# Split products of a two-layer hybrid block: both activation parts in one 512-column product, halves summed by VectorE, and the gated product moved from GpSimd to VectorE

## What is computed

```
for layer in range(2):
    mod = silu(c) @ ada_w[layer] + ada_b[layer]        # six vectors of 2048: shift, scale, gate
    h = rms_norm(x) * (1 + sc_m) + sh_m
    y = even_mixer(h) or odd_mixer(h)                  # projections, mLSTM + forgetting attention, or GLA
    x = x + g_m * rms_norm(y)
    h = rms_norm(x) * (1 + sc_f) + sh_f
    u = conv3(h @ ffn_in_w) + conv_b                   # 2048 -> 2 * 5632, causal depthwise convolution, 3 taps
    a, g = split(u)
    y = (a * gelu(g)) @ ffn_out_w                      # 5632 -> 2048
    x = x + g_f * rms_norm(y)
```

## Time and profile before

| | |
|---|---|
| median of 3 runs | 2530.39 us (2529.86 to 2533.49) |
| the profiled execution | 2531.67 us, its span 2529.9 us |
| mean granted TensorE clock | 0.981 |
| TensorE (PE) busy | 2439.9 us, 96% |
| VectorE (DVE) busy | 1929.7 us, 76% |
| ScalarE (ACT) busy | 999.6 us, 40% |
| GpSimd (POOL) busy | 427.1 us, 17% |
| DMA | 627.17 MB, mean 248 GB/s |

### The profile page before, as it was taken

The page is one execution under the profiler, slowest core; times in us unless marked ns, Lnnn a source line. Parts: engine busy times, 40 slices in busy tenths (PEclk is TensorE's granted clock), DMA queues, the critical chain, the costliest instruction groups (busy, mean ns, idle before and its releaser), DMA issues.

```text
span 2529.9 us, 39852 instructions
## 1 busy us (share of the span) xinstructions
PE 2439.9 (96%) x15954; PEld 2232.7 (88%) x15954; DVE 1929.7 (76%) x2371; ACT 999.6 (40%) x1012; POOL 427.1 (17%) x199
## 2 busy tenths in 40 slices
PE   7999999899999999999999899999999999999998
PEld 5878787789987999799879889987999899988996
DVE  6769888889987999799877676677999466655665
ACT  2133344343333334333444444455433333333343
POOL 0000000014420443024200000000344024410430
PEclk9999999999999999999989999999999999999999
DMA  9989866947788777887858744455677555555553
GB/s 386 412 321 348 311 238 222 325 174 273 273 303 307 277 273 286 323 291 274 302 190 300 241 149 144 149 212 204 250 273 258 194 188 183 182 184 197 181 183 136
DMA packets 114474, 627.17 MB, mean 248 GB/s; under 512 B 12768, under 2 KB 12960, under 8 KB 63152
## 3 DMA queue, kind: packets, MB, share of 16 engines
q1 hardware_dynamic: 113648, 621.22, 67.3%
q10 hardware_dynamic: 704, 4.23, 0.4%
HBM read 623.27 MB, written 2.13 MB: 247 GB/s over the span
## 4 chain that ended last, share of the span: by engine, by line
PE 79%; DVE 10%; DMA 8%; ACT 2%; issue 1%; SPq 0%; DVEq 0%; POOL 0%; ACTq 0%
PE bank L1702 15%; PE bank L1703 15%; PE bank L1704 15%; PE bank L1727 8%; PE bank L1728 8%; PE bank L1729 8%; DMA piece<-ada_pieces 7%; PE bank L1508 4%; DVE lo L920 3%; DVE piece L931 3%; ACT hi L502 1%; PE bank L1614 1%; PE bank L1487 1%; PE bank L1520 1%; DMA extra<-blocks_in 0%
## 5 line engine op out<-in xcount | busy, mean ns | idle before, releaser
L502 ACT ACTIVATE hi<-raw 128x2048 fp32r<-128x2048 f32 x378 | 723.6, 1915 | 1183.8 <-PE bank L1704 734.3
L1702 PE MATMUL bank<-act,hi 128*128 128x256 f32 x3616 | 1032.9, 286 | 12.1 <-DVE lo L920 10.0
L1703 PE MATMUL bank<-act,hi 128*128 128x256 f32 x3616 | 1026.8, 284 | 0.0
L1704 PE MATMUL bank<-act,lo 128*128 128x256 f32 x3616 | 1026.6, 284 | 0.0
L920 DVE TENSOR_TENSOR lo<-raw,hi 128x2048 fp32r<-128x2048 f32 x378 | 864.8, 2288 | 203.5 <-ACT hi L502 202.7
L1702 PEld LDWEIGHTS bank<-act,hi 128*128 128x128 f32 x3616 | 697.8, 193 | 17.8 <-DVE lo L920 12.8
L1703 PEld LDWEIGHTS bank<-act,hi 128*128 128x128 f32 x3616 | 697.7, 193 | 0.3
L1704 PEld LDWEIGHTS bank<-act,lo 128*128 128x128 f32 x3616 | 697.5, 193 | 0.0
L931 DVE SCALAR_TENSOR_TENSOR piece<-piece,cond 128x1024 f32<-128x1024 f32 x290 | 413.8, 1430 | 79.7 <-DMA piece<-ada_pieces 79.5
L901 POOL TENSOR_TENSOR region<-region 128x256 f32<-128x256 f32 x88 | 205.4, 2334 | 1012.4 <-ACT region L805 1012.4
L1727 PE MATMUL bank<-hi,mid 128*128 128x512 f32 x704 | 277.0, 393 | 9.3 <-DVE lo L920 9.3
(11 more groups left out here) (176 smaller groups left out, 1707.6 us busy)
## 6 DMA issues: line engine op xcount, KB each, us to landing
raw<-w_units SPq DMA_DIRECT2D x378, 1024.0 KB, 4.8
piece<-ada_pieces SPq DMA_DIRECT2D x290, 512.0 KB, 4.8
region<-ada_pieces SPq DMA_DIRECT2D x64, 512.0 KB, 11.3
raw<-head_units SPq DMA_DIRECT2D x16, 1024.0 KB, 11.5
y<-ada_pieces SPq DMA_DIRECT2D x30, 512.0 KB, 5.6
region<-gamma_scratch ACTq DMA_DIRECT2D x4, 1024.0 KB, 6.6
x<-x_in SPq DMA_DIRECT2D x1, 2048.0 KB, 9.3
x_out<-x SPq DMA_DIRECT2D x3, 512.0 KB, 2.8
```

The costliest lines, as they stand in the source:

```text
L502: sc.activation(hi[:, slot, :], raw[:, raw_slot, :], ACT.Copy).then_inc(s_hi, 1)
L1702: pe.matmul(dst, w_hi, act[:, kt, 0:T], start=at == 0, stop=False)
L1703: pe.matmul(dst, w_hi, act[:, kt, T:2 * T], start=False, stop=False)
L1704: i_ = pe.matmul(dst, w_lo, act[:, kt, 0:T], start=False, stop=at == DK - 1)
```

## The change

- In all column stages but the gates, L1702 and L1703 become one product with 512 streaming columns, `act[:, kt, :]`, into the whole bank; w_lo x act hi still adds to the first 256 columns.
- The two halves are summed when the bank is evacuated: TENSOR_REDUCE with add over a view of the bank as 256 pairs, each pair 256 elements apart. In the other column stages it takes the place of the copy; in `ff_up` it writes `ff_sum` in SBUF, and the three convolution steps read that in place of the bank, after one more own wait.
- GpSimd's L901 and L904 move to VectorE's queue, behind `lo`: `ff_product` in even iterations, `mid_low` in odd ones, and both behind the first `lo` of the `ff_down` that follows.

```diff
@@ in gpsimd
-                if ph.kind == "ff_up":
-                    def body(i, ph=ph):
...
-                            gp.tensor_tensor(ff_m[:, slot, :], conv_a[:, slot, :], gelu_g[:, slot, :],
-                                             ALU.mult).then_inc(s_mul, 1)
-                            gp.wait_ge(s_mh, p)
-                            gp.tensor_tensor(flat(mid[:, at_, T:2 * T]), ff_m[:, slot, :],
-                                             flat(mid[:, at_, 0:T].bitcast(F32)), ALU.subtract).then_inc(s_mid, 1)
@@ in vector
+            def ff_product(ph, q, slot):
+                ve.wait_ge(s_gelu, ph.pairs + q + 1)
+                if not isinstance(q, int) or ph.pairs + q >= 2:
+                    ve.wait_ge(s_mid, ph.pairs + q - 1)
+                ve.tensor_tensor(ff_m[:, slot, :], conv_a[:, slot, :], gelu_g[:, slot, :], ALU.mult).then_inc(s_mul, 1)
+
+            def mid_low(ph, q, slot):
+                ve.wait_ge(s_mh, ph.pairs + q + 1)
+                at_ = bass.ds(q, 1)
+                ve.tensor_tensor(flat(mid[:, at_, T:2 * T]), ff_m[:, slot, :], flat(mid[:, at_, 0:T].bitcast(F32)),
+                                 ALU.subtract).then_inc(s_mid, 1)
@@ in vector, after lo of the next unit and before the piece
+                        if ph.kind == "ff_up" and not (first_body(i) and j < 2):
+                            q = 2 * i + (j // 2 - 1)
+                            (ff_product if j % 2 == 0 else mid_low)(ph, q, (j // 2 + 1) % 2)
+                        if ph.kind == "ff_down" and first_body(i) and j == 0:
+                            ff_product(last_up, 2 * last_up.bodies - 1, 1)
+                            mid_low(last_up, 2 * last_up.bodies - 1, 1)
@@ in vector, the evacuation
+                        tile_parts = bank[2 * (tile_no % 2)][:, :].rearrange("p (b t) -> p t b", b=2)
...
-                            ve.tensor_copy(region[:, bass.ds((ph.dest + ph.units * i + j) * T, T)], tile_ps)\
-                              .then_inc(s_evac, 1)
+                            ve.tensor_reduce(region[:, bass.ds((ph.dest + ph.units * i + j) * T, T)], tile_parts, AX_X,
+                                             ALU.add).then_inc(s_evac, 1)
...
-                            ve.tensor_scalar(out_, tile_ps, vec[:, bass.ds(ch + 2, 1)], vec[:, bass.ds(ch + 3, 1)],
+                            ve.wait_ge(s_evac, 2 + ph.t0 + i * ph.tiles + tile)
+                            ve.tensor_reduce(ff_sum, tile_parts, AX_X, ALU.add).then_inc(s_v, own.tick())
+                            mine()
+                            ve.tensor_scalar(out_, ff_sum, vec[:, bass.ds(ch + 2, 1)], vec[:, bass.ds(ch + 3, 1)],
                                              ALU.mult, ALU.add).then_inc(s_v, own.tick())
                             mine()
-                            ve.scalar_tensor_tensor(out=out_[:, 1:T], in0=tile_ps[:, 0:T - 1],
+                            ve.scalar_tensor_tensor(out=out_[:, 1:T], in0=ff_sum[:, 0:T - 1],
...
-                            ve.scalar_tensor_tensor(out=out_[:, 2:T], in0=tile_ps[:, 0:T - 2],
+                            ve.scalar_tensor_tensor(out=out_[:, 2:T], in0=ff_sum[:, 0:T - 2],
@@ in tensor, columns
-                    dst = bank[2 * ((ph.t0 + j) % 2)][:, 0:T]
+                    both = bank[2 * ((ph.t0 + j) % 2)][:, :]
+                    dst = both[:, 0:T]
...
-                        pe.matmul(dst, w_hi, act[:, kt, 0:T], start=at == 0, stop=False)
-                        pe.matmul(dst, w_hi, act[:, kt, T:2 * T], start=False, stop=False)
+                        if ph.kind == "gates":
+                            pe.matmul(dst, w_hi, act[:, kt, 0:T], start=at == 0, stop=False)
+                            pe.matmul(dst, w_hi, act[:, kt, T:2 * T], start=False, stop=False)
+                        else:
+
+                            pe.matmul(both, w_hi, act[:, kt, :], start=at == 0, stop=False)
                         i_ = pe.matmul(dst, w_lo, act[:, kt, 0:T], start=False, stop=at == DK - 1)
```

More of the change, by code:

```diff
@@ L175 @@
 REGION = V_AT + TB * D
-OWN = {("ff_up", None): 8, ("columns", "fox"): 6, ("values", "fox"): 12, ("columns", "mlstm"): 14,
+OWN = {("ff_up", None): 12, ("columns", "fox"): 6, ("values", "fox"): 12, ("columns", "mlstm"): 14,
        ("values", "gla"): 8, ("columns", "gla"): 8}
@@ L273, in program @@
                                         for k in range(4))
+        ff_sum = extra[:, 0:T]
         diag = split2(region[:, V_AT:V_AT + T])
@@ L860, in _ @@
             gp.memset(zeros, 0.0).then_inc(s_zeros, 1)
-            gp.sem_inc(s_mul, 2)
             for ph in PHASES:
@@ L894, in _ @@
                         stage_values(h)
-                if ph.kind == "ff_up":
-                    def body(i, ph=ph):
[L897 to L900, removed]
-                            gp.tensor_tensor(ff_m[:, slot, :], conv_a[:, slot, :], gelu_g[:, slot, :],
-                                             ALU.mult).then_inc(s_mul, 1)
-                            gp.wait_ge(s_mh, p)
-                            gp.tensor_tensor(flat(mid[:, at_, T:2 * T]), ff_m[:, slot, :],
-                                             flat(mid[:, at_, 0:T].bitcast(F32)), ALU.subtract).then_inc(s_mid, 1)
-                    repeat(gp, ph, body)
         @block.vector
@@ L1301, in _ @@
             ve.sem_inc(s_pair, 2)
+            ve.sem_inc(s_mul, 2)
             ve.sem_inc(s_mod, 2)
@@ L1469, in _ @@
                     own.at = base + per * ph.bodies
+                if ph.kind == "ff_up":
+                    last_up = ph
                 def between(ph=ph):
```

## The result

| | before | after |
|---|---|---|
| median | 2530.12 us (4 runs, 2528.17 to 2533.49) | 2557.66 us (4 runs, 2554.84 to 2565.55) |
| ratio to before [95% interval] | | 1.0112 [1.0086, 1.0138] |
| the profiled execution, its span | 2531.67, 2529.9 us | 2554.84, 2553.1 us |

The change makes the kernel slower by 27.5 us at the median and by 23.2 us between the two profiled executions, 1.1%. The forecast was 2547.5 us, +17.1, with slower the likeliest: the sign and the mechanism hold, the size was 6 to 10 us short.

The account below looks back on a forecast made before the run. TensorE and VectorE stood within 3% of each other in 120 of 176 `ff_up` units. Terms 27.4 + 0.5 - 11.9 - 3.4 + 2 + 1.5 + 1 gave +17.1 us, a median of 2547.5, range 2533 to 2563.

Parts of the forecast that it names:

- VectorE's cycle: Looped `ff_up` units with a piece: VectorE needs 6.12 us against TensorE's 5.76 before, so +27.4 us over 76 units.
- the piece's stall: VectorE's piece in `ff_up`: 0.54 us of its 1.76 read as waiting for GpSimd, going with GpSimd's work.
- the own wait behind the reduce: VectorE's loops: the one added wait on its own past work lengthens the reduce's 0.69 us by 0.15.
- Straight units: The 44 `ff_up` units with a piece outside loops: VectorE needs 5.77 us, +0.01 each, +0.5 us in all.
- TensorE's part: Column units: one 512-column matmul at 0.227 us replaces two at 0.240, 16 times, saving 0.21 us: 5.55 a unit.
- the 120 units with a piece: `ff_up` units with a piece, looped and straight: VectorE becomes last, +27.9 us forecast.
- the 56 without: `ff_up` units without a piece: TensorE stays last and each saves 0.21 us, -11.9 us.
- Fox and mLSTM: Their 16 column units: engines alternate as last, between -3.4 and +4.3 us, taken as +1.5.
- Rival 1: `ff_up` units with a piece: VectorE's cycle fits under TensorE's and the kernel gets faster, 2495 us; chance 0.15.
- Rival 2: VectorE's convolution steps in `ff_up` cost 0.42 us each from SBUF, giving 2532 us, no change; chance 0.10.
- Rival 3: VectorE's reduce takes two cycles an element for its pairs, 2618 us; chance 0.12, shared with GpSimd's stall not going.
- Rival 4: TensorE's column units: a 512-column product followed by one of 256 costs 0.36 us again, 2563 us; chance 0.03.

## Why the prediction was right, and where its size was off

**VectorE's cycle, 6.12 forecast, 6.17 measured.** Term by term: product 0.34 forecast and measured; piece 1.15 and 1.14; the piece's stall gone with GpSimd's work; TENSOR_REDUCE 0.69 and 0.689; TENSOR_SCALAR from SBUF 0.41 and 0.414; the two steps 0.48 and 0.484. The one miss is the own wait behind the reduce: I gave it the 0.15 of the other two, and it is 0.19 (up to 0.26). 0.05 x 76 units = 3.8 us. Over all loops the mean is 6.20, another 2 us: some units have a longer gap there. Straight units: 5.77 forecast, 5.77 to 5.78 measured.

**TensorE's part was mis-sized:** the step "each replaced two by one, 0.227 against 0.240" priced both products from stretches in which all have one length. Alternating they cost 0.353 a pair in the stages without pieces, so a unit is 5.65 and not 5.55, and 72 units give back 7.9 us instead of 15.3: +7.4. The price of a mixed sequence was no row of before, and I should have carried 0.347 to 0.360 as its bounds.

**The sum with both put right** is 17.1 + 3.8 + 7.4 = 28.3 us, against 27.5 at the medians and 23.2 between the profiled executions. The stages agree less closely than the sum. For the 120 units with a piece +27.9 was forecast, 31.7 with the reduce's wait, and 31.3 measured; but without the first unit of each stage it is 35.3, so that the two figures meet is luck. For the 56 without: -11.9 forecast, -6.2 with the measured pair, -4.4 measured. The 16 column units of GLA, -3.4 forecast, gave -1.2 (-1.8 with the measured pair). Fox and mLSTM, +1.5 forecast in a range from -3.4, came out at -5.1, below that range, and -3.5 of it lies in token units, which the forecast left out: the 8 beside fox take 61.4 us in the kernel before and 57.9 in the changed one. Why they gained was not tried. Decay +2.2 and `ff_down` +1.5 are near the forecast, but no larger than what two traces differ by.

**Rival 1** (VectorE fits, 2495 us) was wrong, but its price of the waits was near: it needed the gaps of 0.15 to vanish, they stayed in the loop, and with straight code they fell to 0.03 to 0.04 and 32 us came back. Even so the unit was 5.77: to reach TensorE's length the sum had to become cheaper as well.

**Rival 2** (convolution steps cheaper from SBUF, 2532 us) was wrong: 0.48 from PSUM in the earlier trace rows, 484 ns from SBUF. The Trainium skill's higher fixed cost of a PSUM source ("VectorE: DVE Perf Modes", "The TRN2 errata") doesn't show in these two steps. TENSOR_SCALAR did gain, 0.54 to 0.41, within 0.01 of what a row of another TENSOR_SCALAR in SBUF had promised.

**Rival 3** (the reduce pays for its pairs) was wrong: 689 ns is that of a reduce over neighbours in SBUF, 686. **Rival 4** (no gain from 512 columns) was half right, as above: in the stages without pieces 0.007 of the 0.013 us is gained, and all of it with the lengths grouped.

## What to carry to other kernels

Before a change takes work from one engine and gives it to another, compare their cycles in each stage by the distance between starts: here 5.76 and 5.6 us stood behind busy shares of 96% and 76%, and the gaps behind an engine's own waits, which no busy share counts, decided. A merged instruction is priced in the sequence it will stand in, not in a run of its own kind. Where a saving is real and the cover is gone, free the other engine: the same 512-column product that cost 1.1% gave 1.5% with the sum split between ScalarE and VectorE, VectorE's code straight and the lengths grouped.

## What the runs showed of the hardware

- **Mixed lengths.** Products of 256 columns cost 0.120 us one behind the other, of 512 columns 0.227; strictly alternating mostly 0.353 a pair, but 0.347 in one stage; two and two 0.693 for both pairs.
- **VectorE and GpSimd hold each other up both ways.** GpSimd's 128x256 product of two SBUF tensors takes 0.74 to 0.88 us when it starts away from `lo` and 2.2 to 2.4 us when it starts under it; the piece that follows on VectorE is then 0.54 longer (1.22 to 1.76). A product that starts away from `lo` lengthens the TENSOR_SCALAR (0.41 to 0.93) or SCALAR_TENSOR_TENSOR (0.48 to 0.73) beside it. In the kernel before this hid in TensorE's shadow: moving the products off GpSimd changed nothing there.
- **An own wait in a loop**, with values and offsets in registers, leaves VectorE idle for 0.15 us behind SCALAR_TENSOR_TENSOR and TENSOR_SCALAR and 0.19 to 0.26 behind TENSOR_REDUCE; in straight code with constants the next instruction starts 0.03 to 0.04 after the record's end.
